# Down pieces of blocks 1 and 2 set between the columns pieces of the next block, and their gated values formed a step sooner

## The reference

```python
def swiglu(x, w_gate, w_up, w_down):
    return (jax.nn.silu(x @ w_gate) * (x @ w_up)) @ w_down
...
    top_vals, top_idx = lax.top_k(logits, TOP_K)
    gates = jax.nn.softmax(top_vals, axis=-1)
    combine = jnp.sum(jax.nn.one_hot(top_idx, N_EXPERTS, dtype=jnp.float32) * gates[..., None], axis=1)
    for e in range(N_EXPERTS):
        y_e = swiglu(xt, w_gate[e], w_up[e], w_down[e])
        y = y + combine[:, e:e + 1] * y_e.astype(jnp.float32)
```

## Time and profile before

| what | us |
|---|---|
| median of 3 runs | 1477.15 (1476.74 to 1477.53) |
| profiled execution | 1477.94 |
| its span | 1476.1 |
| visits, from the first matmul of visit 0 to the end | 609 to 1476 |
| PE busy | 1396.1 (95%) |
| DVE busy | 1334.9 (90%) |
| ACT busy | 1112.9 (75%) |

### The profile page before, as it was taken

One profiled execution on the slowest core, in us unless ns is written; L12 is line 12 of the kernel. 1 busy time (PEld: TensorE's weight loads), 2 busy tenths in 40 slices (PEclk: granted clock), 3 DMA queues, 4 the chain that ended last, 5 costly groups with the idle time before them and its releaser, 6 DMA issues.

```text
span 1476.1 us, 39851 instructions
## 1 busy us (share of the span) xinstructions
PE 1396.1 (95%) x17532; PEld 1150.7 (78%) x17532; DVE 1334.9 (90%) x1351; ACT 1112.9 (75%) x1070; POOL 125.0 (8%) x162
## 2 busy tenths in 40 slices
PE   9999999999999999899999999999999889898786
PEld 7778888888887887788777888787886766766663
DVE  3999999555699999899999999999999999999997
ACT  4697766544478775778888878988887987888884
POOL 2411024000162002100000000000000000000001
PEclk9999999999999999999999999999999999899998
DMA  9645466556464438899999999999999999999993
GB/s 315 248 163 167 162 240 207 192 196 224 151 239 145 164 135 328 318 357 391 411 405 396 411 405 402 411 405 400 410 406 412 411 407 411 410 399 410 411 398 125
DMA packets 141349, 464.86 MB, mean 315 GB/s; under 512 B 8235, under 2 KB 10411, under 8 KB 126801
## 3 DMA queue, kind: packets, MB, share of 16 engines
q1 hardware_dynamic: 138960, 457.21, 81.2%
q0 software_dynamic: 1920, 4.55, 1.0%
q10 hardware_dynamic: 288, 0.48, 0.1%
HBM read 460.79 MB, written 2.89 MB: 314 GB/s over the span
## 4 chain that ended last, share of the span: by engine, by line
PE 55%; DVE 33%; issue 5%; DMA 5%; ACT 2%; SPq 0%; DVEq 0%; ACTq 0%
PE ps L886 17%; PE ps L887 16%; PE ps L888 16%; DVE w_lo L2419 14%; DVE w_lo L2422 6%; DVE w_lo L1841 2%; PE ps L995 2%; ACT w_hi L1750 2%; DMA x<-in_moe_w_gate 2%; DMA stage<-in_w_in 1%; DMA stage<-in_moe_w_up 1%; DVE arena L1989 1%; DVE arena L2000 1%; DVE arena L2437 1%; DVE arena L2457 1%
## 5 line engine op out<-in xcount | busy, mean ns | idle before, releaser
L886 PE MATMUL ps<-arena,w_hi 128*128 128x128 f16 (+8 forms) x4016 | 585.5, 215 | 15.9 <-issue 13.3
L888 PE MATMUL ps<-arena,w_lo 128*128 128x128 f16 (+8 forms) x4016 | 585.3, 215 | 12.9 <-issue 12.9
L887 PE MATMUL ps<-arena,w_hi 128*128 128x128 f16 (+8 forms) x4016 | 585.2, 215 | 7.1 <-issue 7.1
L888 PEld LDWEIGHTS ps<-arena,w_lo 128*128 128x128 f16 x4016 | 394.1, 99 | 26.0 <-issue 19.5
L886 PEld LDWEIGHTS ps<-arena,w_hi 128*128 128x128 f16 x4016 | 394.2, 99 | 20.8 <-issue 10.6
L887 PEld LDWEIGHTS ps<-arena,w_hi 128*128 128x128 f16 x4016 | 394.4, 99 | 18.9 <-issue 9.6
L886 PE MATMUL ps<-xhl,w_hi 128*128 128x264 f16 x1024 | 282.6, 276 | 5.4 <-ACT z L1561 2.0
L888 PE MATMUL ps<-xhl,w_lo 128*128 128x264 f16 x1024 | 282.6, 276 | 0.0
L887 PE MATMUL ps<-xhl,w_hi 128*128 128x264 f16 x1024 | 282.6, 276 | 0.0
L1841 DVE SCALAR_TENSOR_TENSOR w_lo<-stage,w_hi 128x2048 f16<-128x2048 f32 (+1 forms) x94 | 208.9, 2246 | 67.8 <-ACT w_hi L1400 67.7
L2419 DVE SCALAR_TENSOR_TENSOR w_lo<-stage,w_hi 128x2048 f16<-128x2048 f32 x92 | 208.4, 2285 | 13.0 <-ACT w_hi L1750 12.9
(11 more groups left out here) (349 smaller groups left out, 1985.5 us busy)
## 6 DMA issues: line engine op xcount, KB each, us to landing
stage<-in_moe_w_up SPq DMA_DIRECT2D x64, 1024.0 KB, 14.5
stage<-in_moe_w_down SPq DMA_DIRECT2D x48, 1024.0 KB, 14.1
stage<-in_w_in SPq DMA_DIRECT2D x43, 1024.0 KB, 5.3
stage<-in_moe_w_gate SPq DMA_DIRECT2D x34, 1024.0 KB, 9.9
mixer_only<-in_moe_w_up SPq DMA_DIRECT2D x32, 1024.0 KB, 13.7
arena<-in_moe_w_gate SPq DMA_DIRECT2D x32, 1024.0 KB, 13.6
mixer_only<-in_moe_w_gate SPq DMA_DIRECT2D x23, 1024.0 KB, 13.3
mixer_only<-in_moe_w_down SPq DMA_DIRECT2D x16, 1024.0 KB, 14.6
```

Source lines behind the costliest of these rows:

```text
L886: mm(out, ah, bh, start=start, stop=False, skip_group_check=True)
L887: mm(out, ah, bl, start=False, stop=False, skip_group_check=True)
L888: return mm(out, al, bh, start=False, stop=stop, skip_group_check=True)
```

## The change

The order of a visit becomes a function of `MIXED` = 2: blocks 0 and 1 keep their places, and in blocks 2 and 3 one down piece of the block before follows every two (block 2) or every one (block 3) of the columns pieces. With the numbers of the pieces:

g0 u0 (0 to 7), g1 u1 (8 to 15), d0 (16 to 19), g2.0 g2.1 d1.0 g2.2 g2.3 d1.1 u2.0 u2.1 d1.2 u2.2 u2.3 d1.3 (20 to 31), g3.0 d2.0 g3.1 d2.1 u3.0 d2.2 u3.1 d2.3 (32 to 39), d3 (40, 41).

`split_at` gives the last up piece of blocks 1, 2 and 3 one step sooner: the product stands in the step whose number is that of the last up piece, the halves in the next. The special rule for the last visit goes. On PE the pieces from g2.0 to d2.3 are written out by the list; the residual rows that stood behind d1 stand behind g3.1. SP's loads follow the list.

```diff
 def visit_order():
 
     order = []
     for b in range(NB):
-        order += [(kind, b, q) for kind in "gu" for q in range(n_pieces(b))]
-        if b:
-            order += [("d", b - 1, q) for q in range(n_pieces(b - 1))]
+        columns = [(kind, b, q) for kind in "gu" for q in range(n_pieces(b))]
+        rows = [("d", b - 1, q) for q in range(n_pieces(b - 1))] if b else []
+        if b < MIXED:
+            order += columns + rows
+            continue
+        n = len(columns) // len(rows)
+        for i, row in enumerate(rows):
+            order += columns[i * n:(i + 1) * n] + [row]
     return order + [("d", NB - 1, q) for q in range(n_pieces(NB - 1))]
...
             m = q - behind
-            last = max(i for i, p in enumerate(order) if p[0] == "u")
-            if at[1] == NE - 1 and m in (last - 2, last):
-                m = last if m == last - 2 else -1
-            return order[m] if m >= 0 else ("", 0, 0)
+            sooner = order[m + 1] if 0 <= m + 1 < VISIT else ("", 0, 0)
+            if sooner[0] == "u" and sooner[1] >= MIXED - 1 and sooner[2] == n_pieces(sooner[1]) - 1:
+                return sooner
+            found = order[m] if m >= 0 else ("", 0, 0)
+            return found if found[0] != "u" or found[1] < MIXED - 1 else ("", 0, 0)
...
-                for blk in range(2, NB):
-                    gate_up(at, blk)
-                    down(at, blk - 1)
-                    if at[1] == NE - 1 and blk == 2:
+                for m in range(order.index(("g", MIXED, 0)), order.index(("d", NB - 1, 0))):
+                    kind, blk, q = order[m]
+                    if kind == "d":
+                        down(at, blk, [q])
+                    else:
+                        column_piece(at, kind, blk, q)
+                    if at[1] == NE - 1 and (kind, blk, q) == ("g", 3, n_pieces(3) - 1):
                         rows_in(at, 2)
```

More of the change, by code:

```diff
@@ L110, in n_pieces @@
     return 2 * len(BLOCKS[b])
+MIXED = 2
 def visit_order():
@@ L1261, in piece, with column_piece @@
                     t.then_inc(S["part_used"], 1)
+            def column_piece(at, kind, blk, q):
+                if blk == 0 and kind == "g" and q in (0, 2):
+                    for b in ((6, 1), (7, 3))[q // 2]:
+                        pe.wait_ge(*in_visit(bank_free, b, at, -1))
+                piece(at, kind, blk, q)
             def gate_up(at, blk, kinds="gu"):
@@ L1265, in gate_up, with down @@
                     for q in range(n_pieces(blk)):
[L1266 to L1271, removed]
+                        column_piece(at, kind, blk, q)
+            def down(at, blk, pieces=None):
                 cap = CAPS[at[1] % NE]
-                for q in range(n_pieces(blk)):
+                for q in pieces or range(n_pieces(blk)):
                     m = order.index(("d", blk, q))
```

## The result

The changed kernel takes 1516.2 us (median of 4 runs, 1515.92 to 1516.42) against 1477.34 (1476.74 to 1477.53, 4 runs): a ratio of 1.0264, 95% interval 1.0246 to 1.0281, or 38.9 us more. The forecast was 1502, 25 more, in a range of 1490 to 1516: its sign was right, and so were the places at which it had the engines wait; its size was not.

The account below looks back on a forecast made before the run. PE and DVE were taken to limit in turns, with the weight stream ending last. Order terms of 19.2 us plus 6 for the clock, some 25 on the median 1477.15, gave 1502 us, range 1490 to 1516.

Parts of the forecast that it names:

- Cost between 0 (the low stretch lies inside the stall) and 1.7 each: I take 1.0: PE's lower clock behind six stalls, in visits 1 and 3 to 7: 6 us in all, of 0 to 10.2.
- the clock stays low: Rival: each PE stall ends in two low-clock stretches outside it, 3.4 us of loss, 39.6 in all: 1517 us; chance 0.10.
- The order's own cost: All stalls and waits from the new order of pieces, without the clock: 12.0 + 4.4 + 2.6 + 1.4 - 1.2 = 19.2 us.
- Visits 0 to 2: PE's new stalls in visits 0 and 2, 2.6 us; later piece 40 in visit 1, 4.4; late PE slots there, 0.7.
- Visit 3: DVE loses 3.0 us in the passage 3 to 4, plus 0.7 as PE's longer columns pieces free slots late.
- The wait at 39: DVE waits 0.1 us at conversion 39 for ACT's copy, which needs the slot of piece 33.
- Visits 4 to 6: With DVE as the limit, 3.0 us of DVE time lost in each passage to the next visit.
- Conversions 46 and 47: DVE idle 2.5 us before conversion 46, whose copy follows piece 40, and 0.4 before 47, which needs piece 41.
- The stop at 33: PE waits at piece 33 for block 2's low half, behind four conversions: some 8 us at 80 tokens, 5 at 104.
- Visit 7: DVE's 6.1 us of stream waits go, PE ends 5.6 later behind the last conversion, block 3's steps -0.7: sum -1.2.
- Faster: Rival: down pieces spread between light columns pieces let PE catch up at visit 7's end: -2.6, 1474.5 us; chance 0.04.
- Stream hides it: Rival: DVE loses under 6.1 us in all, the last piece lands unchanged, only the tail moves, +1.5: 1479; chance 0.08.

Follow-up runs that it names:

- the kernel with fillers: Changed kernel, with PE running matmuls of 512 columns whose result nobody reads before it waits at piece 33, in visits under 128 tokens: 1501.61 us, ratio 1.0167.
- the kernel with tuned values: Changed kernel, with values of blocks 2 and 3 formed three steps sooner in visits under 128 tokens, one step sooner at 128: 1480.9 us, ratio 1.0023.

## Why the prediction was wrong, by its own steps

The first matmul of each visit against the kernel before, in us, by the windows above and the earlier trace rows; "end" is the last down matmul against the 1458.71 of the earlier trace rows. The forecast's terms are summed up to the same places; "clock kept up" is the kernel with the matmuls in the gap at 33.

| start of | forecast, order alone | measured, clock kept up | forecast, with the clock | changed kernel |
|---|---|---|---|---|
| visit 1 | 1.3 | 1.5 | 1.3 | 1.1 |
| visit 2 | 6.4 | 6.8 | 7.4 | 9.1 |
| visit 3 | 7.7 | 8.6 | 8.7 | 10.9 |
| visit 4 | 11.4 | 14.6 | 13.4 | 19.8 |
| visit 5 | 14.4 | 18.3 | 17.4 | 25.5 |
| visit 6 | 17.4 | 21.7 | 21.4 | 31.0 |
| visit 7 | 20.4 | 24.5 | 25.4 | 37.9 |
| end | 19.2 | 22.2 | 25.2 | 38.1 |

In these executions visit 0 starts 0.5 us (clock kept up) and 0.9 us (changed) earlier than the 609.06 of the kernel before, so visit 0 itself is 2.1 us longer in both.

**The failed step** is "Cost between 0 (the low stretch lies inside the stall) and 1.7 each: I take 1.0". Measured, the clock cost 14.6 us in time, where 6 stood in the sum: 2.0 to 2.6 at the conversion of 39 in each of six visits, and 1.5 once at the conversion of 46. The 1.7 came from one stretch of 3.4 us behind a wait of 3.0; behind PE's idle times of 5.2 to 7.9 us the low clock lasts 6.8 to 10.2 us and reaches 4.0 to 6.1 us past their end (4.2 in visit 5), so that most of the down piece behind, or all of it, runs at the lower level. The upper bound was thus too low. Of the 12.9 us that the last line of the table lacks (38.1 against 25.2), 9.9 are the clock's (15.9 against 6) and 3.0 the order's. The rival "the clock stays low" named the case and got 0.10: it was set aside because low stretches "come singly" in the rows of before, whose waits were shorter. That its 1517 meets the measured time is in part luck: it had 20.4 us for the clock, too much, and 19.2 for the order, too little. By the rule of the Trainium skill, "TensorE: Matmul & The Clock Gate", section "Why this matters for your kernels", every long gap pays, and here the trace agrees: all six did, at 2.0 us or more each. With a conversion more of cover the gap of 5.7 us in visit 5 had the low clock behind it too and cost 0.8 us at 39.

**The order's own cost**, 19.2, measured 22.2 in spans of one execution each (24.7 by the medians of the kernel with fillers, 1501.61 - 1476.94). Visits 0 to 2 are right within 1 us each (2.1 for 1.3, 5.3 for 5.1, 1.8 for 1.3). Visit 3 gave 6.0 us, not 3.7: in the kernel before PE was busy in 102.42 of its 102.80 us and DVE in 102.39, so neither had anything to spare and every stop of PE counted; that reading is argued, not tried apart. The wait at 39 is 0.5 without the clock, where 0.1 stood, 2.4 us over six visits. Visits 4 to 6 gave 3.7, 3.4 and 2.8 for 3.0. That this came out so near is in part luck: the sum did not take off the 0.5 us for which DVE was idle before, and its waits in visit 5 came to 3.7 (0.5 at 39, 2.8 and 0.4 at 46 and 47), not 3.0.

**Conversions 46 and 47**: 2.5 + 0.4 forecast, 2.8 + 0.4 measured (4.4 + 0.5 on the way from visit 6 to 7). **The stop at 33**: 8 us forecast at 80 tokens, 7.9 measured, behind four conversions as read off the order; at 104 tokens 5, and 5.2. **Visit 7**: -1.2 without the clock, -2.3 measured; its 6.1 us of waits for the stream went, 2.1 others came (0.5 at 39, 1.6 at 41), and the last matmul's end is 9.1 us behind the last conversion (1496.82 + 0.22 - 1487.92), not 10.8. **Faster**: in the changed kernel its condition, PE not stopping at 33, was not met; the kernel with tuned values (idle 1.3 us there in visit 5) comes nearest to it, and even there the end came 2.8 us later, not 2.6 sooner. **Stream hides it**: DVE lost far more than the 6.1 us that this asked for.

## What to carry to other kernels

When pieces are put in another order, count for each produced value the work that its producer does, in its own program, between the reader's other inputs and that value: here block 2's low half moved from one conversion ahead of its reader's to three behind it, and block 3's by two conversions, and this cost some 35 us with what followed; one step more in the same direction cost another 48, where in the old order a step gained nothing. Price the stop at the engine that stands still, and then follow the clock: if the piece behind the gap is on the loop, take it at half speed in full, not at a mean of the bounds. And a wait removed at one place (46) comes back at the next (the product) as long as the engine behind it is late by the same amount.

## What the runs showed of the hardware

In visit 5 of the changed kernel the low clock came at 1252.2, 5.2 us into PE's idle time of 7.9, and outlasted it by 4.2 us; behind PE's waits at piece 40 of the changed kernel, 0.5 to 2.2 us, only the longest (visit 6) has a low stretch, of 3.4 us, and DVE's wait at 46 is 4.4 us there, not 2.8; behind each of its six idle times of 5.2 us and more at piece 33 there is one of 6.8 to 10.2. In the kernel with block 2 alone spread, three idle times of 3.1 to 3.7 us have one of 3.4 each behind them, and these cost nothing that the trace shows. Matmuls whose result nobody reads keep the clock at the upper level: the piece behind them took 2.6 us instead of 4.7, and 14.6 of the 38.9 us were gone. They must end before the value that PE waits for is there; where they ended 0.6 to 1.8 us late, the wait behind was longer by as much.
